# Expert weights in pieces of 16 KB to a partition, a ring of eight double places, and normalized rows stored permuted

## The chip, the cores and the metric

The kernel runs on one core of one Trainium2 chip. The metric is the device time of one execution in microseconds.

## The reference, cut to what matters

One transformer layer over 256 tokens of width 2048: three token mixers, a merge with `w_out` (2048 x 2048), a layer norm, a mixture of 16 experts of which each token takes two, and a second layer norm. The change concerns the experts and the first norm.

```python
x = layer_norm(ALPHA * x + mixed @ w_out, ln1_g, ln1_b)          # (256, 2048)
h = silu(einsum('td,edf->etf', x, w_gate)) * einsum('td,edf->etf', x, w_up)   # e = 16, f = 512
h = h * combine.T[:, :, None]                                    # two nonzero experts a token
x = layer_norm(ALPHA * x + einsum('etf,efd->td', h, w_down), ln2_g, ln2_b)
```

Each of `w_gate`, `w_up` (2048 x 512) and `w_down` (512 x 2048) is 4 MB an expert in fp32, so the experts are 192 MB in all (MB is 1,048,576 bytes here and below, where a weight is counted), and every byte is read once.

## The kernel before, in words

The engines run programs of their own and meet at semaphores. SP (`block.sync`) issues nearly all loads, in one fixed order on one queue, and waits before a load until its place is free; so whatever stands behind a waiting load waits too. PE (TensorE) multiplies, ACT (ScalarE) and DVE (VectorE) convert, normalize and add.

**The stages ahead of the experts.** Weights come as units of 1 MB (four rows of 512 columns to a partition, 2 KB each) into a ring `raw` of six slots. ACT rounds a unit to `whi` (line 1619), DVE takes the rest `wlo` (line 1866), PE multiplies three times (lines 1212 to 1214). `lo_done` counts converted units, `unit_used` multiplied ones. `whi` and `wlo` have two slots, so unit u is converted only when unit u - 2 has been multiplied. The 16 units of `w_out` are U1 to U1 + 15 (SP: lines 1093 to 1103, PE: lines 1568 to 1606, where n = u - U1). Between them SP puts in the first expert units, where a place is free by then (`first_units`, lines 406 to 418). DVE adds the residual into `xr` (line 978), storing each 512 columns permuted, so that a partition of a transposed tile holds rows p*4 + k; ACT then normalizes `xr` in place, in two activations (line 674). `gbT` holds the norm's gain and bias, transposed by PE at n = 4 (line 1595).

**The experts.** There are eight pairs of experts, in `step(m)` (line 537); six are written out, one is a loop that runs once with these inputs, and one is the last. An expert pair is 24 units of 1 MB (`expert_unit`, line 355): 16 of gate and up, four rows of 512 columns, which is 8 KB in one piece to a partition, and 8 of down, one row of 2048 columns, 8 KB too. In a pair PE gathers the tokens of both experts, 64 slots each (`gather`, line 510: q is a quarter of the 2048 columns), ACT copies them with gain and bias to `xg` (line 686), `gate_up(q)` (line 556) takes four units for a quarter q, gate and then up, ACT and DVE make `hh`, PE transposes it to `hT` (line 594), and the down product (line 646) takes two units for each quarter f of the 512 rows. `scatter` (lines 522, 523) adds the result of the pair before to the tokens. `m_used` counts used units; the order on PE is gather 0, 1, gate_up 0, gather 2, gate_up 1, gather 3, gate_up 2, 3, down.

**The places.** The first 20 units go to 20 places that come free in the `w_out` stage (`places`, line 231). After that, unit g waits until the unit that had its place before is used (lines 420 to 434). Three of the places (`once`: 14, 15, 16) are not used again, two more (`khT`, `qst`) join once `l1g` and `l1b` are consumed (`start_sum`, line 904), and the ring has 19 places. In the last pair the down units are quarters of columns, with pieces of 2 KB to a partition, and the last two come in halves of 1 KB pieces (`load_last`, line 401; used at line 617). SP's places in the order are lines 395 (a unit), 399 (half of a unit) and 404.

Of the kernel before, what the change touches and what calls it, by code (L numbers as in the profile page):

```python
# [20 lines left out]
P = 128  # L21
# [21 lines left out]
MRAW = 19  # L43
Z = 5
STEPS = 2 * GROUP
MU = 24
# [44 lines left out]
def build(nc, A, out):  # L91
# [14 lines left out]
    with ExitStack() as ctx:  # L106
# [116 lines left out]
        out_acc = at("out_acc", O2, [P, T, D])  # L223
# [10 lines left out]
        once = range(len(places), len(places) + 3)  # L234
        places += [O2, O2 + 8192, made["qbT"]]
        assert made["sig"] + 8192 <= made["cT"] + 2048
        places += [made[name] + (U1 + 15) % SPLIT * 8192 for name in ("whi", "wlo")]
        router_place = len(places)
        places.append(made["sig"])
        NP = len(places)  # L240
        places += [made["khT"], made["qst"]]
        mraw = [at(f"mraw{j}", o, [P, UNIT]) for j, o in enumerate(places)]
        second_round = [j for j in range(NP) if j not in once]
        GROWN = NP + len(second_round)
        ring = second_round[:4] + [NP, NP + 1] + second_round[4:]
        assert len(ring) == MRAW

        def place(g):
            if g < NP:
                return g  # L250
            return second_round[g - NP] if g < GROWN else ring[(g - GROWN) % MRAW]

        def user_before(g):
            return max((e for e in range(g) if place(e) == place(g)), default=None)

        LOOP0, LAST0 = (FIRST * MU - GROWN) % MRAW, (FIRST * MU + MU - GROWN) % MRAW
        L2R = MU - MRAW
        l2g, l2b, ysb = (at(n, places[ring[(LAST0 + L2R + j) % MRAW]], [P, D]) for j, n in enumerate(("l2g", "l2b", "ysb")))
# [28 lines left out]
        gb, gbT = at("gb", made["cT"], [2 * QUADS, 512]), carve(1, "gbT", [P, 2 * KT])  # L287
        wrg, wre = at("wrg", made["ddsa"], [P, KT, NG]), at("wre", made["dist"], [P, KT, NE])
# [9 lines left out]
        def sems(names):  # L298
# [33 lines left out]
        l1_in, l1_var, l1_std, l1_mul, z_ok, acc_ok, gb_in, gb_ps, gb_out = sems(  # L332
            "l1_in l1_var l1_std l1_mul z_ok acc_ok gb_in gb_ps gb_out")
# [21 lines left out]
        def expert_unit(r, pair, quarters=False):  # L355
# [7 lines left out]
            if quarters:  # L363
                c = (r - 4 * QUADS) // 2
                return A["expert_w_down"][0, bass.ds(e, 1), :, c * 512:(c + 1) * 512].rearrange("a (f p) n -> p (a f) n", p=P)
            kf = (r - 4 * QUADS) // 2
            return A["expert_w_down"][0, bass.ds(e, 1), kf * P:(kf + 1) * P, :].rearrange("a p d -> p a d")
# [4 lines left out]
        def loads_of(g):  # L372
            return 2 if NP <= g < NP + 4 else 1

        centre_order = (0, 5, 1, 2, 3, 6, 4, 7)

        def landed_value(r, m, turns):


            if m is not None:  # L380
                g = m * MU + r
                j = place(g)
                return j, mbase[j] + 16 * sum(loads_of(e) for e in range(g + 1) if place(e) == j)
            base = LOOP0 if turns[0] == "loop" else LAST0
            j = ring[(base + r) % MRAW]
            static = sum(loads_of(e) for e in range(FIRST * MU) if place(e) == j)
            turn = sum(1 for e in range(MU) if ring[(LOOP0 + e) % MRAW] == j)
            here = sum(1 for e in range(r + 1) if ring[(base + e) % MRAW] == j)
            return j, mbase[j] + 16 * (static + here) + turns[1] * (16 * turn)

        def load_unit(sp, r, pair, j, quarters=False):
            dst = mraw[j][:].unsqueeze(1)
            if quarters and r >= 4 * QUADS:
                dst = mraw[j][:].rearrange("p (f n) -> p f n", n=512)
            sp.dma_start(dst, expert_unit(r, pair, quarters)).then_inc(mlanded[j], 16)

        def load_half(sp, g, i):
            j, cols = place(g), slice(i * UNIT // 2, (i + 1) * UNIT // 2)
            sp.dma_start(mraw[j][:, cols].unsqueeze(1), expert_unit(g % MU, g // MU)[:, :, cols]).then_inc(mlanded[j], 16)

        def load_last(sp, r, i, signal):
            cols = slice(i * 256, (i + 1) * 256)
            dst = mraw[ring[(LAST0 + r) % MRAW]][:].rearrange("p (f n) -> p f n", n=512)
            sp.dma_start(dst[:, :, cols], expert_unit(r, PAIRS - 1, True)[:, :, cols]).then_inc(signal, 16)

        def first_units(sp, some):
            for r in some:
                if r < 4:
                    sp.wait_ge(unit_used, U1)
                elif r < 6:  # L410
                    sp.wait_ge(m_ps, 8)
                elif r < 6 + RAW:
                    sp.wait_ge(lo_done, U1 + 11 + r - 6)
                elif r == router_place:
# [1196 lines left out]
        def _(act):  # L1611
# [234 lines left out]
            for u in range(U1 + 2, U1 + 16):  # L1846
# [3 lines left out]
                if u == U1 + 2:  # L1850
                    merged(3)
# [295 lines left out]
```

## Time and profile before

| | us |
|---|---|
| median of 3 runs | 1325.91 |
| lowest, highest | 1325.45, 1325.94 |
| the profiled execution | 1324.61 |
| its span | 1322.9 |

PE is busy for 1308.2 us, which is 99% of the span, and its granted clock is full throughout. DVE is busy for 569.2 us and ACT for 476.6 us. The 40 slices of the page are 33 us each; the experts take the last 14. The DMA line is the busy share of the 16 DMA engines in tenths, the GB/s line what they moved. A span of the profiler and the device time of the same execution differ by 1.7 us here, which lies around the span.

### The profile page before, as it was taken

Reading aid. Unit: us, or ns where it says so; the run is one execution under the profiler, and the core shown is the slowest. Engines: PE = TensorE matmul, PEld = TensorE weight load, DVE = VectorE, ACT = ScalarE, POOL = GpSimd, SP = SyncE. Lnnn points to the kernel's source line nnn. Section 1 sums busy time; section 2 is a strip of 40 time slices with the busy share of each in tenths; the row PEclk is TensorE's granted clock in tenths of the full one; section 3 lists DMA queues with packets and bytes.
Section 4 is the critical chain, followed back from the end, with each engine's and each line's share of the span. In section 5 each row is a group of like instructions: output and inputs, shape, how many; then the busy total and the mean of one; then the engine's idle time right before and its main releaser. Section 6 shows DMA issues by size and latency. Waiting matters only on the chain.

```text
span 1322.9 us, 17951 instructions
## 1 busy us (share of the span) xinstructions
PE 1308.2 (99%) x7379; PEld 959.7 (73%) x7379; DVE 569.2 (43%) x741; ACT 476.6 (36%) x667; POOL 29.5 (2%) x55
## 2 busy tenths in 40 slices
PE   9999999999999999999999999999999999999998
PEld 9999989998888888888888888844453444544443
DVE  4367445356555644464455555525112121221206
ACT  4535343346556544454333433422121121211212
POOL 1000000400000000000100001000000000000000
PEclk9999999999999999999999999999999999999999
DMA  9965555544454445554556795699999999999996
GB/s 302 344 230 197 175 190 188 190 160 160 159 161 156 160 154 194 174 174 159 191 190 226 262 393 178 264 416 416 422 420 422 420 421 421 421 421 420 422 408 253
DMA packets 122100, 364.97 MB, mean 276 GB/s; under 512 B 11627, under 2 KB 19243, under 8 KB 98486
## 3 DMA queue, kind: packets, MB, share of 16 engines
q1 hardware_dynamic: 115430, 359.06, 73.1%
q10 hardware_dynamic: 6608, 5.02, 1.3%
q8 instruction: 47, 0.77, 0.2%
q14 instruction: 15, 0.12, 0.0%
HBM read 361.96 MB, written 2.10 MB: 275 GB/s over the span
## 4 chain that ended last, share of the span: by engine, by line
PE 93%; DMA 3%; DVE 2%; ACT 0%; issue 0%; SPq 0%; DVEq 0%; ACTq 0%
PE main L1212 19%; PE main L1214 19%; PE main L1213 19%; PE main L556 16%; PE att L646 7%; PE att L510 5%; DMA mraw<-in_expert_w_down_dram 3%; PE att L1453 1%; PE main L522 1%; PE main L523 1%; PE att L1436 1%; PE att L1472 1%; PE att L1468 1%; DVE wlo L1866 1%; PE att L1423 0%; PE att L617 0%
## 5 line engine op out<-in xcount | busy, mean ns | idle before, releaser
L1866 DVE TENSOR_TENSOR wlo<-raw,whi 128x2048 fp32r<-128x2048 f32 x135 | 310.3, 2299 | 360.3 <-ACT whi L1619 360.3
L1619 ACT ACTIVATE whi<-raw 128x2048 fp32r<-128x2048 f32 x135 | 258.1, 1912 | 420.4 <-PE main L1214 418.9
L556 PE MATMUL main<-mraw,xg 128*64 128x512 f32 x1024 | 225.4, 595 | 1.5 <-DMA mraw<-in_expert_w_up_dram 1.4
L1212 PE MATMUL main<-whi,xhi 128*128 128x512 f32 (+1 forms) x544 | 203.9, 375 | 0.0
L1214 PE MATMUL main<-whi,xlo 128*128 128x512 f32 (+1 forms) x544 | 201.7, 371 | 0.0
L1213 PE MATMUL main<-wlo,xhi 128*128 128x512 f32 (+1 forms) x544 | 201.6, 371 | 0.0
L556 PEld LDWEIGHTS main<-mraw,xg 128*64 128x64 f32 x1024 | 72.1, 137 | 137.4 <-issue 136.2
L1212 PE MATMUL main<-xhi,whi 128*128 128x256 f32 (+1 forms) x560 | 159.6, 285 | 1.1 <-DVE wlo L1997 1.0
L1213 PE MATMUL main<-xlo,whi 128*128 128x256 f32 (+1 forms) x560 | 158.4, 283 | 0.0
L1214 PE MATMUL main<-xhi,wlo 128*128 128x256 f32 (+1 forms) x560 | 158.4, 283 | 0.0
L1214 PEld LDWEIGHTS main<-whi,xlo 128*128 128x128 f32 x544 | 102.5, 188 | 17.7
L1213 PEld LDWEIGHTS main<-wlo,xhi 128*128 128x128 f32 x544 | 102.6, 189 | 17.2
L1212 PEld LDWEIGHTS main<-whi,xhi 128*128 128x128 f32 x544 | 102.6, 189 | 17.1
L1212 PEld LDWEIGHTS main<-xhi,whi 128*128 128x128 f32 (+1 forms) x560 | 106.9, 191 | 2.7 <-DVE xlo L1988 1.2
L1213 PEld LDWEIGHTS main<-xlo,whi 128*128 128x128 f32 (+1 forms) x560 | 106.9, 191 | 0.0
L1214 PEld LDWEIGHTS main<-xhi,wlo 128*128 128x128 f32 (+1 forms) x560 | 106.9, 191 | 0.0
L646 PE MATMUL att<-mraw,hT 128*64 128x512 f32 x448 | 98.1, 594 | 3.1 <-DMA mraw<-in_expert_w_down_dram 2.4
L686 ACT ACTIVATE xg<-att,gbT 128x128 f32<-128x128 f32 x128 | 47.3, 465 | 124.8 <-PE att L510 124.4
L646 PEld LDWEIGHTS att<-mraw,hT 128*64 128x64 f32 x448 | 31.6, 137 | 65.1 <-issue 60.9
L1212 PE MATMUL main<-whi,o 128*128 128x512 f32 x192 | 76.4, 398 | 0.0
L1214 PE MATMUL main<-whi,o 128*128 128x512 f32 x192 | 75.0, 391 | 0.0
L1213 PE MATMUL main<-wlo,o 128*128 128x512 f32 x192 | 74.8, 389 | 0.0
(336 smaller groups left out, 1300.8 us busy)
## 6 DMA issues: line engine op xcount, KB each, us to landing
raw<-in_w_in_dram SPq DMA_DIRECT2D x95, 1024.0 KB, 5.1
mraw<-in_expert_w_gate_dram SPq DMA_DIRECT2D x64, 1024.0 KB, 21.3
mraw<-in_expert_w_up_dram SPq DMA_DIRECT2D x64, 1024.0 KB, 22.4
mraw<-in_expert_w_down_dram SPq DMA_DIRECT2D x58, 1024.0 KB, 23.1
raw<-in_w_branch_dram SPq DMA_DIRECT2D x24, 1024.0 KB, 5.0
raw<-in_w_out_dram SPq DMA_DIRECT2D x16, 1024.0 KB, 7.9
mraw<-in_expert_w_down_dram SPq DMA_DIRECT2D x12, 512.0 KB, 9.3
xin<-in_x_dram SPq DMA_DIRECT2D x4, 512.0 KB, 8.2
```

What stands on the lines that cost most here:

```text
L510: ins = pe.matmul(att[:, q, k % 4 * P:(k % 4 + 1) * P], xr[:, t, k * P:(k + 1) * P], hot[:, t, :], start=(k % 4 == 0 and t == 0), stop=(t ...
L522: pe.matmul(o, rows, yhi[:, c % 2, :], start=True, stop=False)
L523: pe.matmul(o, rows, ylo[:, c % 2, :], start=False, stop=True).then_inc(sc_ps, 1)
L556: ins = pe.matmul(main[0][half, w, :], xg[:, k, half], src[:, kk * DE:(kk + 1) * DE], start=(k == 0), stop=(k == KT - 1))
L646: ins = pe.matmul(att[half, c, :], hT[:, f, half], src[:, c * 512:(c + 1) * 512], start=(f == 0), stop=(f == DE // P - 1))
L686: ins = act.activation(xg[:, k, :], att[:, q, k % 4 * P:(k % 4 + 1) * P], ACT.Identity, bias=gbT[:, KT + k:KT + k + 1], scale=gbT[:, k:k + 1])
L1212: pe.matmul(o, ah, bh, start=start, stop=False, skip_group_check=skip)
L1213: pe.matmul(o, ah, bl, start=False, stop=False, skip_group_check=skip)
L1214: return pe.matmul(o, al, bh, start=False, stop=stop, skip_group_check=skip)
L1436: ins = pe.transpose(att[:, seg, blk * P:(blk + 1) * P], sP[:, seg, blk * P:(blk + 1) * P], ident[:])
L1619: act.activation(whi[:, u % SPLIT, 0:n], raw[:, slot, 0:n], ACT.Copy).then_inc(hi_done, 1)
L1866: dve.tensor_tensor(wlo[:, u % SPLIT, 0:n], raw[:, slot, 0:n], whi[:, u % SPLIT, 0:n].bitcast(F32), ALU.subtract).then_inc(lo_done, 1)
```

## The change

An expert unit is now 2 MB: eight rows of 512 columns to a partition for gate and up, two rows of 2048 columns for down, in one piece of 16 KB. A pair has 12 units (`MU`), 8 of them gate and up (`GU`). The ring has eight double places; a double place is two of the old ones that lie side by side. `khT`, `qst`, the place at `sig` and the one at `qbT` are no longer in the ring. The first ten units fill the same 20 MB as before: five of them, and the first two of the ring's second turn, come in halves of 8 KB pieces (`load_half`), and unit 7 goes to where `xr` was, after the norm.

A unit of eight rows to a partition needs tokens in another order. ACT therefore normalizes `xr` into a new tensor `xn` (at the place of `mhi`), in eight activations of 512 columns that read with a stride; `out_acc` lies where `xr` was; and a second transposed gain and bias, `gbX`, is made: two small loads on SP ahead of U1 + 6, eight transposes on PE at n = 8, one copy on ACT. The small tensor `gbx` lies in place 5, so SP waits for the transposes before it loads unit 2. In a pair PE now uses all of gate before all of up within a half h: `gate_up(0)`, gather 2, gather 3, `gate_up(1)`. The down quarters of the last pair keep their shape.

```diff
-MRAW = 19
+RING = 8
-MU = 24
+MU = 12
+GU = 8
...
+        ring = [(0, 1), (2, 3), (4, 5), *((raw_at[n], raw_at[n + 1]) for n in range(0, RAW, 2)), *w_at]
+        first = [*ring[:7], (14, 15), ring[7], (16, 19)]
...
         def place(g):
-            if g < NP:
-                return g
-            return second_round[g - NP] if g < GROWN else ring[(g - GROWN) % MRAW]
+            return first[g] if g < NF else ring[(g - NF) % RING]
...
-            if r < 4 * QUADS:
-                q, name = r // 4, ("expert_w_gate", "expert_w_up")[r % 4 // 2]
-                rows = A[name][0, bass.ds(e, 1), q * 512:(q + 1) * 512, :]
+            if r < GU:
+                h, name = r // 4, ("expert_w_gate", "expert_w_up")[r % 4 // 2]
+                rows = A[name][0, bass.ds(e, 1), h * 1024:(h + 1) * 1024, :]
...
+            sp.wait_ge(z_ok, 2 * QUADS)
+            load_unit(sp, 7, 0, place(7))
+            sp.wait_ge(lt_out, 3)
+            for g in (NF, NF + 1):
+                load_half(sp, g, 0)
+            for g in (NF, NF + 1):
+                sp.wait_ge(m_used, user_before(g) + 1)
+                load_half(sp, g, 1)
+            for g in range(NF + 2, FIRST * MU):
+                sp.wait_ge(m_used, user_before(g) + 1)
                 load_unit(sp, g % MU, g // MU, place(g))
...
+                def gate_up(h):
+
                     for w in range(2):
+                        for kk in range(8):
+                            k = 8 * h + kk
+                            if kk % 4 == 0:
+                                if w == 0:
+                                    pe.wait_ge(xg_out, 1 + k // 4 + m * 4)
+                                for a in range(2):
+                                    arrived(4 * h + 2 * w + a, kk // 4)
...
-                                if kk == 3:
+                                if kk == 7:
                                     ins.then_inc(m_used, 1)
-                                elif kk == 1 and fixed == 0 and q == 0:
+                                elif kk == 3 and fixed == 0 and h == 0 and w == 0:
                                     ins.then_inc(lt_out, 1)
...
-                            if c == 3:
+                            if c == 3 and f % 2:
                                 ins.then_inc(m_used, 1)
...
-            for t in range(T):
-                act.activation(xr[:, t, :], xr[:, t, :], ACT.Identity, bias=nmr[:, t:t + 1],
-                               scale=rstd[:, t:t + 1]).then_inc(z_ok, 1)
+            for q in range(4):
+                half = slice(q // 2 * 1024, (q // 2 + 1) * 1024)
+                for t in range(T):
+                    src = xr[:, t, half].rearrange("p (c k m b) -> p b k c m", c=2, k=4, b=2)[:, q % 2]
+                    act.activation(xn[:, t, q * 512:(q + 1) * 512].rearrange("p (k c m) -> p k c m", k=4, c=2), src, ACT.Identity,
+                                   bias=nmr[:, t:t + 1], scale=rstd[:, t:t + 1]).then_inc(z_ok, 1)
...
+                    if u == U1 + 6:
+                        sp.wait_ge(m_ps, 8)
+                        for j, name in enumerate(("ln1_g", "ln1_b")):
+                            sp.dma_start(gbx[2 * j:2 * j + 2, :], A[name][0].rearrange("(h n) -> h n", h=2)).then_inc(gbx_in, 16)
                     if u in (U1 + 7, U1 + 9, U1 + 11):
-                        first_units(sp, range(u - U1 - 7, u - U1 - 5))
+                        g = (u - U1 - 7) // 2
+                        sp.wait_ge(unit_used, U1)
+                        if g == 2:
+                            sp.wait_ge(gb_ps, 2)
+                        load_unit(sp, g, 0, place(g))
...
+                    if n == 8:
+                        pe.wait_ge(gbx_in, 32)
+                        pe.wait_ge(gb_out, 1)
+                        for k in range(8):
+                            ins = pe.transpose(att[:, 2, 128 + k * 4:128 + (k + 1) * 4],
+                                               gbx[:].rearrange("r (m k) -> r k m", k=8)[:, k, :], ident[0:4, 0:4])
+                        ins.then_inc(gb_ps, 1)
```

Two places of the order show what moves. The first is SP's queue in the `w_out` stage, ahead of and behind the load of the unit at U1 + 11; `mraw` and `mtwo` are the old and the double places, `raw` the ring of the `w_out` units. Before:

```order
L395 DMA mraw_136<-in_expert_w_up_dram 128x2048 [waits unit_used]
L395 DMA mraw_137<-in_expert_w_up_dram 128x2048 [waits unit_used]
L1048 DMA raw<-in_w_out_dram 128x4x512 [waits lo_done] x2
L395 DMA mraw_138<-in_expert_w_gate_dram 128x2048 [waits m_ps]
L395 DMA mraw_139<-in_expert_w_gate_dram 128x2048 [waits m_ps]
L1048 DMA raw<-in_w_out_dram 128x4x512 [waits lo_done] x5
```

After the change:

```order
L1132 DMA gbx<-in_ln_g_dram 2x1024 [waits m_ps]
L1132 DMA gbx<-in_ln_b_dram 2x1024
L1077 DMA raw<-in_w_out_dram 128x4x512 [waits lo_done]
L402 DMA mtwo_143<-in_expert_w_gate_dram 128x4096 [waits unit_used]
L1077 DMA raw<-in_w_out_dram 128x4x512 [waits lo_done] x2
L402 DMA mtwo_144<-in_expert_w_gate_dram 128x4096 [waits unit_used]
L1077 DMA raw<-in_w_out_dram 128x4x512 [waits lo_done] x2
L402 DMA mtwo_145<-in_expert_w_up_dram 128x4096 [waits gb_ps,unit_used]
L1077 DMA raw<-in_w_out_dram 128x4x512 [waits lo_done] x5
```

The five last `w_out` loads now stand behind a load that waits for `gb_ps`, which PE raises to 2 behind its eight new transposes at n = 8; before, the load ahead of them waited for `m_ps` alone.

The second place is SP's queue at the start of the experts, from the first load that waits for a multiply of the experts. Before:

```order
L399 DMA mraw_134<-in_expert_w_down_dram 128x1024 [waits lt_out]
L399 DMA mraw_135<-in_expert_w_down_dram 128x1024 [waits lt_out]
L399 DMA mraw_134<-in_expert_w_down_dram 128x1024 [waits m_used]
L399 DMA mraw_135<-in_expert_w_down_dram 128x1024 [waits m_used]
L399 DMA mraw_136<-in_expert_w_down_dram 128x1024 [waits lt_out]
L399 DMA mraw_137<-in_expert_w_down_dram 128x1024 [waits lt_out]
L399 DMA mraw_136<-in_expert_w_down_dram 128x1024 [waits m_used]
L399 DMA mraw_137<-in_expert_w_down_dram 128x1024 [waits m_used]
L395 DMA mraw_138<-in_expert_w_gate_dram 128x2048 [waits m_used]
L395 DMA mraw_139<-in_expert_w_gate_dram 128x2048 [waits m_used]
```

After the change:

```order
L402 DMA mtwo_150<-in_expert_w_up_dram 128x4096 [waits z_ok]
L406 DMA mtwo_143<-in_expert_w_down_dram 128x2048 [waits lt_out]
L406 DMA mtwo_144<-in_expert_w_down_dram 128x2048
L406 DMA mtwo_143<-in_expert_w_down_dram 128x2048 [waits m_used]
L406 DMA mtwo_144<-in_expert_w_down_dram 128x2048 [waits m_used]
L402 DMA mtwo_145<-in_expert_w_gate_dram 128x4096 [waits m_used]
L402 DMA mtwo_146<-in_expert_w_gate_dram 128x4096 [waits m_used]
```

The waits are of the same kind, but each now stands for twice the bytes, and `m_used` is raised half as often.

## Rows read from the trace of the kernel before

**Rows 1.** The page: GB/s in 40 slices; DMA issues, KB each, median us to landing.

```profile
GB/s 302 344 230 197 175 190 188 190 160 160 159 161 156 160 154 194 174 174 159 191 190 226 262 393 178 264 416 416 422 420 422 420 421 421 421 421 420 422 408 253
...
mraw<-in_expert_w_gate_dram SPq DMA_DIRECT2D x64, 1024.0 KB, 21.3
...
raw<-in_w_branch_dram SPq DMA_DIRECT2D x24, 1024.0 KB, 5.0
```

**Rows 2.** Windows: PE, PEld, DVE, ACT, POOL busy (instructions), PEclk, DMA share, GB/s.

```profile
868.00:1280.00 412.00, 407.66 (x2102) 183.08 (x2098) 84.92 (x169) 73.63 (x193) 0.00 (x0) 1.00 1.01 420
1060.00:1160.00 100.00, 99.83 (x522) 45.99 (x520) 21.10 (x46) 20.12 (x52) 0.00 (x0) 1.00 1.01 421
1286.00:1292.00 6.00, 4.97 (x23) 1.84 (x21) 2.02 (x4) 1.46 (x5) 0.00 (x0) 1.00 1.05 387
```

**Rows 3.** Waits of PE from 820 us on: engine, line, releaser, us, times, longest.

```profile
PE att L646 <- DMA mraw<-in_expert_w_down_dram: 2.4, 2, 1.4
PE att L617 <- DMA mraw<-in_expert_w_down_dram: 1.4, 2, 0.9
PE main L556 <- DMA mraw<-in_expert_w_up_dram: 1.4, 1, 1.4
```

**Rows 4.** Chain of waits, first two pairs: start, us, engine, tile, line, count.

```profile
863.63 7.02 PE main L556 x32
870.65 1.98 PE att L510 x16
872.63 7.02 PE main L556 x32
...
882.19 13.93 PE main L556 x64
...
898.08 13.95 PE att L646 x64
...
918.57 7.02 PE main L556 x32
```

**Rows 5.** Timeline of SP's DMA issues around the last `w_out` units: start, span, count.

```profile
784.99 23.81 SPq L1048 DMA_DIRECT2D raw<-in_w_out_dram  x5
813.95 6.51 SPq L395 DMA_DIRECT2D mraw<-in_expert_w_up_dram  x2
...
852.09 0.81 SPq L395 DMA_DIRECT2D mraw<-in_expert_w_up_dram  x2
852.94 3.07 SPq L395 DMA_DIRECT2D mraw<-in_expert_w_down_dram  x4
```

**Rows 6.** Chain of waits in the `w_out` stage: start, us, engine, tile, line, count.

```profile
786.07 0.57 PE att L1595 x4
...
809.51 0.57 PE att L1561 x8
...
821.20 0.87 PE att L1552 x8
```

**Rows 7.** Timeline of ACT and of DVE: conversion of unit U1 + 10.

```profile
809.61 1.92 ACT L1619 ACTIVATE whi<-raw 128x2048 fp32r<-128x2048 f32 x1 [3.52 <-PE main L1214]
...
811.64 2.27 DVE L1866 TENSOR_TENSOR wlo<-raw,whi 128x2048 fp32r<-128x2048 f32 x1
```

**Rows 8.** Timeline of ACT ahead of the first pair: normalization, tables, first `xg`.

```profile
855.20 4.08 ACT L674 ACTIVATE xr<-xr,nmr,rstd 128x2048 f32<-128x2048 f32 x2 [0.43 <-DVE nmr L1017]
...
861.88 1.50 ACT L686 ACTIVATE xg<-att,gbT 128x128 f32<-128x128 f32 x4 [0.82 <-PE att L510]
```

**Rows 9.** Timeline of PE in the last pair, from its last gate/up units on.

```profile
1281.83 3.65 PE L556 MATMUL main<-mraw,xg 128*64 128x512 f32 x16 [1.36 <-DMA mraw<-in_expert_w_up_dram]
...
1288.12 3.65 PE L617 MATMUL att<-mraw,hT 128*64 128x512 f32 x16 [0.80 <-ACT hT L702]
1292.68 3.65 PE L617 MATMUL att<-mraw,hT 128*64 128x512 f32 x16 [0.91 <-DMA mraw<-in_expert_w_down_dram]
...
1297.98 3.65 PE L617 MATMUL att<-mraw,hT 128*64 128x512 f32 x16 [0.51 <-DMA mraw<-in_expert_w_down_dram]
```

More of the change, by code:

```diff
@@ L242, in build @@
[L242 to L246, printed above, removed]
+        raw_at = {(places[j] - made["raw"]) // 8192: j for j in range(6, 6 + RAW)}
+        w_at = [(12, 17), (13, 18)] if places[12] < places[17] else [(17, 12), (18, 13)]
+        ring = [(0, 1), (2, 3), (4, 5), *((raw_at[n], raw_at[n + 1]) for n in range(0, RAW, 2)), *w_at]
@@ new lines, in build, with half_of @@
+        first = [*ring[:7], (14, 15), ring[7], (16, 19)]
+        assert len(ring) == RING and all(places[a] + 8192 == places[b] for a, b in ring + first[:9])
+        NF = len(first)
+        IN_HALVES = (5, 6, 8, 9, NF, NF + 1)
+        doubles = {a: at(f"mtwo{a}", places[a], [P, 2 * UNIT]) for a, _ in ring + first[:9]}
+        singles = [at(f"mraw{j}", places[j], [P, UNIT]) for j in first[9]]
+        def half_of(where, i):
+            return singles[i][:] if where == first[9] else doubles[where[0]][:, i * UNIT:(i + 1) * UNIT]
@@ L248, in place @@
         def place(g):
-            if g < NP:
-                return g
-            return second_round[g - NP] if g < GROWN else ring[(g - GROWN) % MRAW]
+            return first[g] if g < NF else ring[(g - NF) % RING]
         def user_before(g):
[L254 to L258, printed above, removed]
+            return max(e for e in range(g) if place(e) == place(g))
@@ L259, in build @@
+        LOOP0, LAST0 = (FIRST * MU - NF) % RING, (FIRST * MU + MU - NF) % RING
+        L2R = GU // 2
+        l2g, l2b, ysb = (at(n, places[j], [P, D]) for n, j in zip(
+            ("l2g", "l2b", "ysb"), (*ring[(LAST0 + L2R) % RING], ring[(LAST0 + L2R + 1) % RING][0])))
         small = [made["ksT"], made["pT"]]
@@ L380, in landed_value @@
+        def landed_value(r, m, turns, half):
             if m is not None:
                 g = m * MU + r
[L382 to L387, printed above, removed]
@@ L401, in load_last @@
[L401 to L414, printed above, removed]
-                    sp.wait_ge(r_ps, T)
-                else:
-                    sp.wait_ge(unit_used, U1 + 4 * QUADS - (1 if r < 8 + RAW else 0))
-                load_unit(sp, r, 0, r)
@@ new lines, in landed_value @@
+                return j, mbase[j] + 16 * sum(signals(e, j) for e in range(g + 1))
+            last = turns[0] == "last"
+            base = LAST0 if last else LOOP0
+            j = ring[(base + r) % RING][half if last and r >= GU else 0]
+            static = sum(signals(e, j) for e in range(FIRST * MU))
+            turn = sum(1 for e in range(MU) if ring[(LOOP0 + e) % RING][0] == j)
+            here = sum(1 for e in range(r + 1) if ring[(base + e) % RING][half if last and e >= GU else 0] == j)
@@ new lines, in tile, with arrived @@
+                def tile(r, half):
+                    if fixed is not None:
+                        return half_of(place(fixed * MU + r), half)
+                    return half_of(ring[((LAST0 if turns[0] == "last" else LOOP0) + r) % RING], half)
+                def arrived(r, half):
+                    if half == 0 or (fixed is not None and fixed * MU + r in IN_HALVES):
+                        landed_, value = unit(r, half)
+                        pe.wait_ge(landed_, value)
+                def gate_up(h):
+                    for w in range(2):
+                        for kk in range(8):
[3 more added lines that the diff above has]
+                                    pe.wait_ge(xg_out, 1 + k // 4 + m * 4)
+                                for a in range(2):
+                                    arrived(4 * h + 2 * w + a, kk // 4)
```

169 lines of the change are left out of this document (87 added, 82 removed).

## The prediction

> **What bounds the kernel now.** I read the DMA line of the page first. Its last 14 slices are the experts, and from the 27th on it stands at 416 to 422 GB/s, where the stages before move 154 to 393 [rows 1]. The windows say the same in one number: from 868 to 1280 us the DMA engines are at a share of 1.01 and move 420 GB/s, 421 in the middle [rows 2]. But PE is busy for 407.7 of the same 412 us. The waits of PE decide between the two: from 820 us on PE waits for weights five times, 5.2 us in all, all of it late (up units, down units, last quarters) [rows 3]. The chain of waits gives the pace of PE: a pair begins `gate_up(0)` at 863.63, the next at 918.57, so a pair needs 54.9 us of PE [rows 4]. A pair is 24 MB; at 421 GB/s that is 24 x 2.491 = 59.8 us of DMA. **So the stage is bound by DMA, and PE lives for five pairs on the 20 MB loaded ahead of it.** The DMA queue never ran dry: a unit lands 21.3 us after its issue, against the 2.5 us that it takes [rows 1]. The last gate/up unit lands at 1281.83, and behind it the quarters come so closely that PE waits before the second and the third [rows 9]. What happens to DMA between about 868 and 1282 is therefore what the change is worth, plus what it puts on PE ahead of that.
>
> A difference below 0.2% (2.65 us) can't be told from no change here.
>
> **Term 1, the piece of 16 KB.** Pieces of 8 KB run at 421 GB/s and those of 2 KB in the last pair at 387 [rows 2]. By engine that is 16 x 8192 / 421 = 311.3 ns and 16 x 2048 / 387 = 84.7 ns a piece: 36.9 ns for each 1000 bytes and 9.2 ns fixed. A piece of 16 KB should take 613.4 ns, against 622.6 for two, which is 427 GB/s and 0.037 us less a MB. Bounds: nothing (a long piece is cut in two, or costs in proportion), and the rate with no fixed cost at all, 434 GB/s (0.075 us a MB). I take the fit, since it goes through the nearest rows. Of the 164 MB that come after the first 20 and up to the last gate/up unit, 160 have 16 KB pieces: 160 x 0.037 = **-5.9 us** (0 to -12).
>
> The Trainium skill (DMA: Bandwidth & Descriptors, Why small descriptors are slow) gives the fixed cost as about 3 cycles a packet, and elsewhere on the page a fabric clock of 850 MHz, which makes an estimate of 3.5 ns; the rows above show 9.2. By the page's figure this term would be -2.3 us and the sum 3.6 us higher; the measured one decides.
>
> **Term 2, the queue runs dry.** A load waits until its place is used. Before, places of 1 MB come free two at a time each 3.5 us, of 19. Now they come free 4 MB at a time each 7 us, of 16, and unit 7, the one at `sig` and the one at `qbT` are out of the ring. I walk through the first two pairs in the time of before. PE's marks are from the chain [rows 4]: `gate_up(0)` from 863.63 for 14.04 (both old parts), `gate_up(1)` from 882.19 for 13.93, down from 898.08 for 13.95, next pair from 918.57. A place is known free 0.13 us after the multiply (865.38 by the chain, 865.52 on SP). A load on an empty queue starts 1.0 us later: a 1 MB unit lands 5.0 us after its issue [rows 1] and takes 2.7 at 2 KB pieces, so 2.3 us lie at its two ends, of which I give the start a bit less than half (0 to 2.3). It shifts every restart alike and changes the sum of the gaps little. A MB takes 2.52 us over the whole stretch (164 MB from 868.2 to 1281.83; the code loads and restarts are in it), so with the new pieces 2.483, and a double unit 4.97.
>
> The first 20 MB end at 868.2, as before: three units from 852.09 on, a fourth with `r_ps`, and unit 7 behind the norm (about 860) still find the queue busy until then [rows 5, 8]. Then, with the release and the start of each:
> - units 10, 11, first halves: released at 867.14, start 868.3, gap 0.2; with the second halves (870.65) they end at 878.4.
> - 12, 13: released at 877.67 (up used), start 878.8, gap 0.4, end 888.7.
> - 14, 15: 889.16, start 890.3, gap 1.6, end 900.2. Unit 16 (896.12): no gap, end 905.2.
> - 17: waits for down, 905.05, gap 1.0, end 911.2.
> - 18, 19: 912.03, gap 2.0, end 923.1.
> - 20, 21: 925.59, gap 3.6, end 936.6. From 22 on (932.6) the releases lead, since PE is the faster.
>
> Sum: **+8.8 us** of lost DMA time, which a stage bound by DMA never gets back. PE doesn't feel it there: units 12, 13 are needed at 918.57. Bounds: 0, if the places come as early as before; 12, if each of the six restarts costs 0.5 us more.
>
> **Term 3, the w_out stage.** PE has eight more transposes at n = 8. Four cost 0.57 us [rows 6], so +1.1. And SP now waits for them before unit 2 and the five last `w_out` loads. Before, these five were issued from 784.99 on, though the first of them (U1 + 11) is needed late [rows 5]. Now: n = 8 ends at 809.51 [rows 6], the transposes at 810.65, unit 2 starts at 811.8 and takes 4.9, the unit U1 + 11 takes 2.7 at 387 GB/s and lands at 819.4; ACT needs 1.92, DVE 2.27 [rows 7], so PE can start n = 11 at 823.8. It would be there at 822.07 (821.20 + 0.87) + 1.1 = 823.2 [rows 6]. That is +0.6, **together +1.8** with 0.1 for two more semaphores. Both shift the later marks of PE, the releases and the DMA alike. Bounds: +1.1 and, if the load is 3 us later than I reckon, +4.7. The wait for `m_ps` ahead of U1 + 6 holds loads that have 20 us to spare.
>
> **Term 4, the end.** PE takes 7.0 us for up of both experts after the last 4 MB have landed, not 3.65 for the last 2 MB [rows 9]: +3.35. In exchange the waits before the second and third quarter, 0.9 and 0.5, vanish, for the quarters land 5.4 us apart: **+1.9**. Bounds: 0 and 3.4.
>
> **Edits at nothing.** The norm in eight pieces: 4.08 us as two [rows 8], perhaps 4.7 as eight, until 859.9; the first gather waits for the token table and starts at 859.86 in any case, and ACT has 0.8 us free before its first `xg` [rows 8]. If the stride cost double, PE would be late by about 3 us once. The other order of gather 3, the strided transposes of `hh`, `gbX`, the sum in four pieces on DVE: beside a busy PE, or four small weight loads a pair. Half as many issues on SP: it waits anyway.
>
> **Sum:** -5.9 + 8.8 + 1.8 + 1.9 = +6.6 us. The profiled execution (1324.61, span 1322.9) would go to 1331.2, span 1329.5; the median shown is 1.3 us above it, so 1325.91 + 6.6 = 1332.5.
>
> **Rivals.**
> - *The piece of 16 KB brings nothing.* Term 1 is 0, the gaps shrink by 0.6: 1337.8. For: no load of before has such a piece. Against: the fixed cost shows from 2 to 8 KB. 17%.
> - *The queue doesn't run dry.* If releases or starts come sooner, so that the gaps stay near zero, as before, term 1 wins: 1332.5 - 8.8 = 1323.7, the border of faster. It decides from a gap sum below about 0.3 us. Against: the rows of the chain leave no room for six such gaps to close. 12%.
> - *A transfer of double size runs much faster,* and DMA is no longer the bound. Then PE waits for nothing: -6.2 (the 5.2 of rows 3 and what follows from them in the last two pairs) + 1.8 = -4.4, 1321.5. This needs over 439 GB/s from a fit that ends at 434, or both this and smaller gaps. 6%.
> - *The late `w_out` load costs more* (upper bound of term 3): 1335.4. 8%.
> - *Terms cancel:* gaps half as long, rest as reckoned: about 1328. 7%.
>
> The third is what a rule of the Trainium skill would give (the same page, Bandwidth: batch to at least 1 MB, 78% of the peak there and 97% at 16 MB); the 21.3 us in the queue against 2.5 us of moving show that the fixed cost of a load is hidden already.
>
> **Numbers.** The forecast has 50%, its own range is 1329 to 1336. The range of 8 in 10 takes in the first rival, and the second in part: 1325 to 1339. Faster by over 0.2% (below 1323.3): the third rival and half of the second, 12%. Within 0.2%: the rest of the second, the last one, 15%. Slower: 73%.
>
> **What would show it.** DMA share below 1 in windows between 878 and 927, later at 1.01 with about 427 GB/s; a wait of PE before n = 11; waits for weights already in the sixth pair; seven us of up after the last wait for gate/up. Wrong if the GB/s line holds 420 or more from the start of the experts on, or if the rate of the middle is 421 or less.

## The result, and the profile after

| us | before | after |
|---|---|---|
| median | 1325.80 (4 runs) | 1336.32 (4 runs) |
| lowest, highest | 1325.45, 1325.94 | 1336.04, 1336.93 |
| the profiled execution | 1324.61 | 1336.19 |
| its span | 1322.9 | 1334.5 |

The changed kernel is slower by 10.5 us: the ratio is 1.008, with a 95% interval from 1.0063 to 1.0098. The forecast was 1332.5 with a range of 1325 to 1339. The sign and this range hold; the narrower one, 1329 to 1336, is missed by 0.3, and the sum of +6.6 is 3.9 us short. I look for those 3.9 us first, and then ask whether the terms that fit the total also fit their places.

**The rate.** Two lines of the page after (GB/s in 40 slices of 33.4 us; a gate load with KB and us to landing), to be held against [rows 1]:

```profile
GB/s 305 345 219 205 177 192 188 170 170 165 164 163 145 169 157 158 183 194 156 190 189 258 193 280 258 311 380 351 423 428 427 427 427 429 426 427 428 426 410 225
...
mtwo<-in_expert_w_gate_dram SPq DMA_DIRECT2D x31, 2048.0 KB, 22.1
```

The middle of the experts runs at 426 to 429 GB/s where it ran at 420 to 422, and ahead of it stand a 380, a 351 and a 423 where before had 416, 416 and 422. Windows put the same in stretches of equal length. The window of before over its first 70 us of the experts (us; PE, PEld, DVE, ACT, POOL busy; PEclk; DMA share; GB/s):

```profile
863.00:933.00 70.00, 68.82 (x358) 30.40 (x358) 23.88 (x43) 14.92 (x39) 0.00 (x0) 1.00 1.01 417
```

and those of the changed kernel: the same stretch of its experts, the middle, and some short ones to which I come below.

```profile
870.00:940.00 70.00, 68.38 (x351) 29.72 (x352) 23.62 (x39) 13.31 (x35) 0.00 (x0) 1.00 0.93 365
1060.00:1160.00 100.00, 97.96 (x495) 43.83 (x492) 19.05 (x37) 17.04 (x43) 0.00 (x0) 1.00 1.01 428
...
810.88:812.88 2.00, 2.00 (x15) 1.32 (x8) 2.00 (x3) 0.95 (x1) 0.00 (x0) 1.00 0.68 123
812.88:814.88 2.00, 2.00 (x11) 1.65 (x10) 1.37 (x1) 0.00 (x0) 0.00 (x0) 1.00 0.85 344
810.88:822.15 11.27, 11.27 (x56) 9.00 (x49) 3.37 (x3) 0.95 (x1) 0.00 (x0) 1.00 0.91 339
...
826.00:830.00 4.00, 3.55 (x10) 2.86 (x11) 3.59 (x4) 1.68 (x2) 0.00 (x0) 0.59 1.05 388
...
1252.00:1254.00 2.00, 2.00 (x9) 0.78 (x7) 0.00 (x0) 0.00 (x0) 0.00 (x0) 0.64 1.04 442
1254.00:1256.00 2.00, 2.00 (x6) 0.61 (x4) 0.00 (x0) 0.00 (x0) 0.00 (x0) 0.51 0.96 410
```

The DMA share falls to 0.93 in the first 70 us. At 417 GB/s instead of 365, 3.64 million bytes more would have gone through, which is 8.7 us of DMA; term 2, the dry queue, had 8.8. And 428 against 421 is term 1: 0.04 us a MB.

**The w_out stage.** The waits of PE from 700 us on (engine, line, releaser: us, times, longest):

```profile
PE att L672 <- DMA mtwo<-in_expert_w_down_dram: 8.9, 5, 2.8
PE main L1249 <- DVE wlo L1915: 3.1, 1, 3.1
PE main L581 <- DMA mtwo<-in_expert_w_up_dram: 1.7, 1, 1.7
...
PE main L581 <- ACT xg L715: 0.9, 1, 0.9
```

The second row is new: PE stands still for 3.1 us before n = 11, in a stage that had no such wait in [rows 3]. The chain of waits tells how it came about (start, us, engine, tile, line, count):

```profile
809.82 0.98 PE att L1639 x8
810.88 0.34 SPq L402
811.26 10.87 DMA raw<-in_w_out_dram
822.15 1.93 ACT whi L1663
824.10 2.30 DVE wlo L1915
826.45 0.80 PE main L1249
827.24 0.43 PE main L1250
827.67 0.43 PE main L1251
...
870.44 13.96 PE main L581 x64
```

It reads from the top: the eight new transposes (0.98), SP's issue of unit 2, then the load of the `w_out` unit U1 + 11, which lands 10.87 us after 811.26; ACT and DVE convert it in 4.3 us; PE goes on at 826.45. And the matmuls behind it stand 0.43 us apart, where the same three lines stand 0.23 apart before the wait: the window from 826 to 830 has a granted clock of 0.59, after PE had been idle for 3.1 us. That is the lower level of 1.2 GHz for most of the stretch, where before had the full clock throughout. The Trainium skill (TensorE: Matmul & The Clock Gate, Wait — 56ns, not 53.3ns?) gives 426.7 ns from matmul to matmul at 512 columns and 1.2 GHz; the 0.43 agrees.

On SP the wait that causes it has a row of its own (queue, line, releaser: us, times, longest):

```profile
SPq L1137 <- PE att L1639: 30.6, 1, 30.6
```

SP has nothing to do for 30.6 us but wait for the transposes. Of the five loads behind it, four have time; U1 + 11 has not. The activations of the norm in the same kernel (timeline of ACT):

```profile
861.20 6.09 ACT L703 ACTIVATE xn<-xr,nmr,rstd 128x512 f32<-128x512 f32 x8 [0.43 <-DVE nmr L1046]
```

take 6.09 us as eight, where two took 4.08 [rows 8], and PE waits 0.9 for the first `xg`.

**The end.** The timeline of PE in the changed kernel, seventh and last pair:

```profile
1251.38 8.78 PE L672 MATMUL att<-mtwo,hT 128*64 128x512 f32 x32 [2.70 <-DMA mtwo<-in_expert_w_down_dram]
...
1284.84 13.95 PE L581 MATMUL main<-mtwo,xg 128*64 128x512 f32 x64
```

Thirty-two matmuls take 8.78 us instead of the 7.09 that this group takes elsewhere. The windows from 1252 to 1256 say why: granted clock 0.64 and 0.51, after an idle time of 2.70. In the last pair PE then finds the 64 gate/up matmuls of its second half all supplied.

### The profile page after: what moved, and what is told of

It reads as the page before. It is cut to its first block, busy times and chain, and to the rows that moved or that the text cites. A ratio compares the mean times of both kernels' runs of the same rounds, so it can differ in the third digit from the quotient of the medians.

```text
span 1334.5 us, 17804 instructions
## 1 busy us (share of the span) xinstructions
PE 1310.8 (98%) x7387; PEld 967.7 (73%) x7387; DVE 569.1 (43%) x737; ACT 478.4 (36%) x674; POOL 29.5 (2%) x55
## 4 chain that ended last, share of the span: by engine, by line
PE 88%; DMA 8%; DVE 2%; ACT 1%; issue 0%; SPq 0%; DVEq 0%; ACTq 0%
PE main L1249 19%; PE main L1251 18%; PE main L1250 18%; PE main L581 14%; DMA mtwo<-in_expert_w_down_dram 7%; PE att L672 6%; PE att L524 3%; PE att L1490 1%; PE main L536 1%; PE att L644 1%; PE main L537 1%; DMA raw<-in_w_out_dram 1%; DVE wlo L1915 1%; PE att L1473 1%; PE att L1509 1%; PE att L1505 1%
## 5 line engine op out<-in xcount | busy, mean ns | idle before, releaser
L581 PE MATMUL main<-mtwo,xg 128*64 128x512 f32 x1024 | 223.8, 594 | 2.9 <-DMA mtwo<-in_expert_w_up_dram 1.7
L581 PEld LDWEIGHTS main<-mtwo,xg 128*64 128x64 f32 x1024 | 74.1, 137 | 141.3 <-issue 140.1
L672 PE MATMUL att<-mtwo,hT 128*64 128x512 f32 x432 | 100.0, 603 | 9.3 <-DMA mtwo<-in_expert_w_down_dram 8.9
L715 ACT ACTIVATE xg<-att,gbX 128x128 f32<-128x128 f32 x128 | 47.2, 464 | 121.3 <-PE att L524 120.9
L672 PEld LDWEIGHTS att<-mtwo,hT 128*64 128x64 f32 x432 | 33.9, 139 | 70.5 <-issue 67.3
```

The source lines that it names most:

```text
L581: ins = pe.matmul(main[0][half, w, :], xg[:, k, half], src[:, kk % 4 * DE:(kk % 4 + 1) * DE], start=(k == 0), stop=(k == KT - 1))
L672: ins = pe.matmul(att[half, c, :], hT[:, f, half], src[:, c * 512:(c + 1) * 512], start=(f == 0), stop=(f == DE // P - 1))
L715: ins = act.activation(xg[:, k, :], att[:, q, k % 4 * P:(k % 4 + 1) * P], ACT.Identity, bias=gbX[:, KT + k:KT + k + 1], scale=gbX[:, k:k + 1])
```

## The experiments

Nine kernels were run, one of them twice, each beside the kernel before on the same chip, whose medians were 1325.65, 1325.51 and 1325.57 in the three groups of runs. My theory was that the total is made of the four terms, with term 3 larger than I had put it and the clock as its hidden part; the rivals were a slower norm, a useless piece size, and a queue that fell dry for another reason than places and releases.

**1. Unit 2 later: the wait off the path.** SP loads unit 2, and waits for the transposes, only behind the last `w_out` load.

```diff
         def moe_loads(sp):
+            sp.wait_ge(gb_ps, 2)
+            load_unit(sp, 2, 0, place(2))
             sp.wait_ge(lo_done, U1 + 11)
...
-                    if u in (U1 + 7, U1 + 9, U1 + 11):
+                    if u in (U1 + 7, U1 + 9):
...
-                        if g == 2:
-                            sp.wait_ge(gb_ps, 2)
```

> The changed kernel, with the load of expert unit 2 and its wait for the new transposes put behind the last w_out load instead of ahead of five of them. Theory (SP's wait holds the w_out weights; what PE loses there is lost to the end, since the release of places and the norm shift with it): the wait of PE of 3.1 us before n = 11 goes, and so do the slow matmuls behind it (about 1.4 us); the first gate product starts near 866 instead of 870.4; time 1336.3 - 4.5 = 1331.8. Rival (the experts are bound by DMA, so a late start of PE costs nothing while DMA is fed): 1336. Second rival (loading unit 2 later only moves the loss): above 1335, with a late unit 2 or a longer dry queue.

Measured: 1330.93 (1329.96 to 1331.38), ratio 1.0042 (1.0028 to 1.0056); run once more in a later group it gave 1330.09 (1329.82 to 1330.67), ratio 1.0036 (1.0022 to 1.0050).

> The kernel of e1_unit2_late once more, on the same chip as e5_late_flat, to compare the two directly. 1330.9 as before, by every theory; a difference of more than 1 us would say how far runs on another chip carry.

The wait for `wlo` is gone, the first gate product starts at 865.63 instead of 870.44, and the first 70 us still run at 366 GB/s:

```profile
865.00:935.00 70.00, 68.20 (x349) 29.59 (x350) 23.79 (x40) 13.49 (x35) 0.00 (x0) 1.00 0.93 366
```

So the order of SP's loads in the `w_out` stage costs about half of what the change costs, and the dry queue has nothing to do with it. The timeline of PE shows the end of this kernel too:

```profile
1187.51 8.78 PE L674 MATMUL att<-mtwo,hT 128*64 128x512 f32 x32 [2.92 <-DMA mtwo<-in_expert_w_down_dram]
...
1246.24 7.09 PE L674 MATMUL att<-mtwo,hT 128*64 128x512 f32 x32 [2.04 <-DMA mtwo<-in_expert_w_down_dram]
...
1285.46 7.09 PE L583 MATMUL main<-mtwo,xg 128*64 128x512 f32 x32 [0.33 <-DMA mtwo<-in_expert_w_up_dram]
```

The first row is the low clock again, behind a wait of 2.92 us; it cost nothing there, since PE had to wait for the next down units all the same (2.04). Here PE does wait in the last pair's up, and has 7.09 us of it after the last 4 MB have landed. From that mark to the end of the span (1328.2) there are 42.7 us; before, from 1281.83 [rows 9] to 1322.9, there were 41.1. That is term 4, +1.7 for a forecast of +1.9, where it was said to be.

**2. The same wait in the kernel before.** Only this is added to before:

```diff
                             sp.dma_start(x_of(j), A["x"][0, :, j * 512:(j + 1) * 512].rearrange("(t p) d -> p t d", p=P)).then_inc(xr_in, 16)
+                    if u == U1 + 11:
+                        sp.wait_ge(unit_used, U1 + 9)
```

> The kernel before with one wait added: SP waits until PE has done n = 8 before it loads units 4, 5 and the w_out unit U1 + 11. Theory (the wait alone makes PE wait about 3 us before n = 11 and then run about 1.4 us at the lower clock, and this is lost to the end): 1325.8 + 4.4 = 1330.2. Rival (DMA bound, a late PE costs nothing): 1325.8. Rival (the later loads of units 4 and 5 also hold the next loads): above 1332.

Measured: 1330.75 (1329.38 to 1331.41), ratio 1.0038 (1.0025 to 1.0052). The windows, then the chain of waits of this kernel:

```profile
809.63:811.63 2.00, 2.00 (x15) 1.32 (x16) 1.97 (x3) 1.92 (x1) 0.00 (x0) 1.00 0.43 78
811.63:813.63 2.00, 2.00 (x10) 1.66 (x9) 2.00 (x2) 0.00 (x0) 0.00 (x0) 1.00 1.00 414
...
826.00:830.00 4.00, 4.00 (x11) 3.17 (x10) 3.29 (x3) 0.53 (x1) 0.00 (x0) 0.50 1.08 399
870.00:940.00 70.00, 68.82 (x356) 30.08 (x354) 23.14 (x39) 14.41 (x37) 0.00 (x0) 1.00 1.01 415
```

```profile
825.28 0.80 PE main L1214
826.07 0.43 PE main L1215
...
831.16 0.23 PE main L1215
...
869.81 7.02 PE main L556 x32
```

One wait on SP, with no other part of the change, moves the first gate product by 6.2 us (863.63 in [rows 4]) and the time by 5.1. The profiled execution is one of the longer ones: its span is 6.6 us over that of before. By the timeline, from the first matmul of n = 11 to the fifteenth pass 6.0 us here (825.28 to 831.23) and 3.3 in before (821.83 to 825.10). So the clock adds 2.7 us to an idle time of the same 3.1 us as in the changed kernel, where it added 1.4 (3.3 us from the first to the ninth, 1.9 in before). The DMA share is 1.01 in the first 70 us: no dry queue with 19 fine places.

**3. Pieces of 8 KB in the changed kernel.** Each 2 MB unit is loaded by two DMAs of 8 KB pieces to the same place; the counts of landed loads follow.

```diff
...
-            sp.dma_start(doubles[where[0]][:].unsqueeze(1), expert_unit(r, pair)).then_inc(mlanded[where[0]], 16)
+            for i in range(2):
+                cols = slice(i * UNIT, (i + 1) * UNIT)
+                sp.dma_start(half_of(where, i).unsqueeze(1), expert_unit(r, pair)[:, :, cols]).then_inc(mlanded[where[0]], 16)
```

> The changed kernel with each 2 MB unit loaded by two DMAs with pieces of 8 KB; places, waits and order unchanged. Theory (a piece has a fixed cost of about 9 ns, worth 0.037 us a MB): rate in the middle 421 GB/s instead of 428, the units of the last pairs land 5 to 6 us later, time 1341.5. Rival (the size of the piece has no part in it): 1336.3. Rival the other way (smaller loads fill the queue better at the start and win back some of the gaps): 1334 to 1336.

Measured: 1340.58 (1340.01 to 1341.06), ratio 1.0113 (1.0097 to 1.0128); that is 0.0033 above the changed kernel's ratio, 4.4 us.

```profile
870.00:940.00 70.00, 68.19 (x349) 29.56 (x350) 23.79 (x40) 13.49 (x35) 0.00 (x0) 1.00 0.93 366
1060.00:1160.00 100.00, 94.80 (x479) 43.24 (x477) 19.07 (x37) 17.05 (x43) 0.00 (x0) 1.00 1.01 422
```

The rate of the middle goes back to 422, while the first 70 us move 366 GB/s as with long pieces: where the queue waits for places, the long piece gains nothing. And PE's waits for down and up grow from 8.9 and 1.7 to 11.5 and 3.5. The long piece is worth what the two rates say: 160 MB x 0.035 us is 5.6, of which 4.4 to 4.8 (spans 1339.3 against 1334.5) arrive. The first rival is out.

**4. Sixteen places, release by fours, and both, in the kernel before.** First `MRAW = 16`, with the ring's list cut accordingly (`ring = second_round`); then 19 places, but a load waits until the group of four units is used:

```diff
-                    sp.wait_ge(m_used, user_before(g) + 1)
+                    sp.wait_ge(m_used, user_before(g) // 4 * 4 + 4)
```

and then both.

> The kernel before with a ring of 16 places of 1 MB instead of 19 (the place at sig is used once, khT and qst never). Theory (capacity alone makes the DMA queue run dry in the first two pairs): gaps of 4.6 us in sum, the largest near 920 us, none after 930; time 1325.7 + 4.4 = 1330.1. Rival (the gaps of the change come from places being given back 4 MB at a time alone): no gap, 1325.7.

> The kernel before with its 19 places, but from the fifth unit behind the first 20 on SP waits until all four units of a quarter (or of two down rows) are used, so places come free 4 MB at a time. Theory (coarse release alone costs gaps too, but less than half): gaps of 2.7 us near 880 and 906 us, time 1325.7 + 2.5 = 1328.2. Rival (release alone is the cause): 1334. Rival (19 places hide it): 1325.7.

> The kernel before with both: 16 places and release by fours; pieces stay at 8 KB and the w_out stage is untouched. Theory (capacity and release together are the changed kernel's dry queue): gaps of 8.1 us, time 1325.7 + 7.9 = 1333.6, more than either alone. Rival (the two overlap, the larger one decides): 1330.

Measured: 1328.73 (1328.25 to 1329.29), ratio 1.0025 (1.0015 to 1.0035); 1328.31 (1327.74 to 1329.60), ratio 1.0021 (1.0012 to 1.0031); both together 1333.62 (1331.93 to 1334.57), ratio 1.0057 (1.0044 to 1.0071). The windows over the first 70 us of sixteen places:

```profile
864.00:934.00 70.00, 68.82 (x356) 30.09 (x356) 23.24 (x40) 14.48 (x37) 0.00 (x0) 1.00 0.97 390
```

of release by fours:

```profile
864.00:934.00 70.00, 68.82 (x356) 30.13 (x356) 23.47 (x41) 14.53 (x37) 0.00 (x0) 1.00 0.99 395
```

and of both:

```profile
863.00:933.00 70.00, 68.82 (x359) 30.52 (x359) 23.94 (x43) 15.04 (x39) 0.00 (x0) 1.00 0.93 369
```

Against 417 these are 4.5, 3.7 and 8.1 us of DMA, where I expected gaps of 4.6, 2.7 and 8.1; the time of sixteen places, expected at 1330.1, came out 1.4 us lower. In the timeline the last down product of the seventh pair starts at 1241.13 in before, at 1245.73, 1245.39 and 1250.91 here: +4.6, +4.3 and +9.8, so what the queue loses stands whole at that mark. In the windows the two losses add (4.5 + 3.7 against 8.1); at the mark and in the time both together cost more than the sum of the single ones (9.8 against 8.9, and 8.1 against 6.0). About half of the latter has a reason. Of a loss about 1 us is not seen in the time (+3.2 and +2.8 for the single ones), because before itself loses about 1 us between that mark and the last up units: 40.7 us pass between the two there (1241.13 to 1281.83), 39.75 with sixteen places (to 1285.48). That 1 us is hidden twice in the sum of the single ones and once in both together; the rest of the difference stays open. The dry queue is thus half capacity, half granularity, and with both it is nearly as large as in the changed kernel (8.1 against 8.7).

**5. Release by halves in the changed kernel.** Experiment 1, and the first 16 units of the ring's turns come in halves of 8 KB pieces, each loaded when its half of the place is used (a new semaphore `half_used` at the fourth of eight steps).

```diff
-        IN_HALVES = (5, 6, 8, 9, NF, NF + 1)
+        IN_HALVES = (5, 6, 8, 9, *range(NF, NF + 16))
...
+            for g0 in range(NF, NF + 16, 2):
+                for i, used in enumerate((half_used, m_used)):
+                    for g in (g0, g0 + 1):
+                        sp.wait_ge(used, user_before(g) + 1)
+                        load_half(sp, g, i)
```

> The changed kernel with unit 2 loaded late (as e1_unit2_late), and in the first two pairs of the ring (units 10 to 25) loads of 1 MB that start as soon as half a unit is used; from unit 26 on double units as in the change. Theory (finer release fills about half of the gaps, for 32 MB at the 8 KB rate): gaps 4.7 instead of about 8.8 us, time 1330.9 - 3.1 = 1327.8. Rival (capacity alone counts): 1331. Rival (twice the waits and issues on SP eat it): above 1331.

Measured: 1327.79 (1326.76 to 1329.45), ratio 1.0017 (1.0008 to 1.0026).

```profile
865.00:935.00 70.00, 68.39 (x351) 29.72 (x352) 23.61 (x39) 13.34 (x35) 0.00 (x0) 1.00 0.96 385
1060.00:1160.00 100.00, 99.83 (x522) 46.65 (x520) 21.11 (x46) 20.16 (x52) 0.00 (x0) 1.00 1.01 428
```

385 instead of 366 GB/s is 3.2 us of DMA, and 3.1 are gone from the time (2.3 by the second run of experiment 1). The middle keeps its 428, since long pieces matter only where the queue is full. What is left of the gaps is 5.4 us by the window; sixteen places alone cost 4.5 in experiment 4, and the rest I did not take apart. This is the fastest version of the changed kernel that I ran, and before is still faster by 2.3 us.

**6. The norm without the permutation.** Eight activations of 512 columns, read and written in order, once in the changed kernel and once on top of experiment 1. The result is then not the layer's, since the columns of the tokens meet the wrong weight rows; the loads and multiplies stay the same.

```diff
-                half = slice(q // 2 * 1024, (q // 2 + 1) * 1024)
+                cols = slice(q * 512, (q + 1) * 512)
...
-                    act.activation(xn[:, t, q * 512:(q + 1) * 512].rearrange("p (k c m) -> p k c m", k=4, c=2), src, ACT.Identity,
+                    act.activation(xn[:, t, cols], xr[:, t, cols], ACT.Identity,
```

> The changed kernel, with the eight activations of the norm reading and writing 512 columns in a row, without the permutation (so the columns of the tokens meet the wrong weight rows; all else as before). Theory (the strided read costs ACT 160 ns an activation, and PE 0.9 us at the first gate product): each activation 0.6 us instead of 0.76, the eight 4.8 instead of 6.1, no wait of PE for xg, time 1335.4. Rival (hidden, since DMA bounds): 1336.3. Other rival (the norm's end also holds unit 7, so more): 1334.5.

> e1_unit2_late and e2_flat_norm together: unit 2 loaded behind the last w_out load, and the norm without the permutation (the columns of the tokens meet the wrong weight rows). It asks again what the strided norm costs, without the wait of PE in the w_out stage, which alone varied by 1.1 us between the profiles. Theory (the stride costs PE 0.9 us at the first gate product and nothing later): 1330.9 - 0.9 = 1330.0, no wait for xg. Rival (hidden, since DMA bounds): 1330.9. Rival (the norm's end also delays unit 7 and with it the queue): 1329.

Measured: 1335.48 (1332.81 to 1336.65), ratio 1.0071 (1.0057 to 1.0085), and 1329.65 (1329.41 to 1331.19), ratio 1.0035 (1.0023 to 1.0048), beside 1330.09 for experiment 1 on the same chip. The timeline of ACT in the second of them:

```profile
856.38 5.75 ACT L704 ACTIVATE xn<-xr,nmr,rstd 128x512 f32<-128x512 f32 x8 [0.43 <-DVE nmr L1047]
```

The stride costs 0.34 us in all, the cutting into eight 1.67 (5.75 against 4.08). I had expected 160 ns an activation for the stride; it is 43 ns. PE still waits 0.53 us for `xg`, 0.3 less than with the stride, and the 0.4 us between the medians can't be told from the spread of the runs. The first of the two is inconclusive as a time, and that it met the expected 1335.4 is luck: its wait before n = 11 was 4.2 us in the profiled execution, and its runs spread over 3.8 us. But its timeline of PE has two rows that matter for the clock and the end:

```profile
1252.80 7.09 PE L672 MATMUL att<-mtwo,hT 128*64 128x512 f32 x32 [2.70 <-DMA mtwo<-in_expert_w_down_dram]
...
1292.03 7.09 PE L581 MATMUL main<-mtwo,xg 128*64 128x512 f32 x32 [0.36 <-DMA mtwo<-in_expert_w_up_dram]
```

The same wait as in the changed kernel at the same place, 2.70 us, and the clock stayed full; 39.2 us later the last up units have landed, as in experiment 1 (1246.24 to 1285.46), and PE has waited for them.

## Why the prediction was right or wrong

**What bounds the kernel: right.** Every DMA loss that I made stood whole at the end of the seventh pair (experiment 4), and of the 5.6 us of rate taken away in experiment 3, 4.4 to 4.8 came out in the time. The signs named came too: the DMA share fell, PE waited before n = 11, and it waited for weights even a pair earlier than said, in the fifth (at 1132.34).

**Term 1, the piece of 16 KB, -5.9: right.** 428 GB/s against a forecast of 427, or 612.5 ns a piece against 613.4; taken away, it costs 4.4 to 4.8 us. The fixed cost that I fitted from pieces of 2 and 8 KB, 9.2 ns, holds at 16. The 3 cycles of the Trainium skill (DMA: Bandwidth & Descriptors, Why small descriptors are slow), 3.5 ns in my estimate, would have made the term -2.3; experiment 3 decides for the fit.

**Term 2, the dry queue, +8.8: right,** 8.7 by the windows. The cause was also the one of the walk, too few places and too coarse releases, each of which gives about half alone. The places of the gaps fit as well: the widest one of the walk, from 923.1 to 926.7, moved by the 6.8 us that PE is later, is 929.9 to 933.5, and the windows of the changed kernel there are

```profile
928.44:930.44 2.00, 2.00 (x12) 0.69 (x10) 0.00 (x0) 0.00 (x0) 0.00 (x0) 1.00 0.83 352
930.44:932.44 2.00, 2.00 (x12) 0.60 (x10) 0.00 (x0) 0.00 (x0) 0.00 (x0) 1.00 0.08 33
932.44:934.44 2.00, 2.00 (x12) 0.72 (x10) 0.00 (x0) 0.00 (x0) 0.00 (x0) 1.00 0.80 156
```

The second rival (no gaps) is out.

**Term 3, the w_out stage, is the step that failed: "+0.6, together +1.8" is 6.8.** The first gate product starts at 870.44 and not 863.63. By the chain: 0.3 was there already ahead of the stage (786.38 for the transposes at n = 4, against 786.07); the eight transposes are 1.0, as forecast (1.1); the wait for `wlo` puts n = 11 another 3.3 us later, where I had 0.6; the low clock behind it adds 1.4, where I had nothing; the norm and the wait for `xg` add 0.8, which I had under "edits at nothing" as 0.6 us of ACT that would hide.

Two sizes are wrong. First, the landing of U1 + 11: I had unit 2 and the next load run at full rate from the first microsecond (819.4). It landed at 822.15. The idle queue started slowly: 123 and 344 GB/s in the first four microseconds, against some 420 that is 1.8 us of DMA, of which I had 0.9. And by 822.15 DMA had moved 3.6 MB (339 GB/s for 11.27 us), though unit 2 and U1 + 11 are 3: the loads issued behind U1 + 11 took their share of the engines before it was complete. Second, I priced a wait of PE by its length alone. A full-clock kernel has no row that shows what PE does after an idle time of 3 us, and I didn't ask what it would cost if the clock fell. The range did hold "the load 3 us later", +4.7, as the fourth rival; with the clock and the norm behind it, it is 6.8. Experiment 2 shows the wait and the clock of this term without the transposes and the norm, at +5.1 in time; experiment 1 takes these two away, 4.8 us at the first gate product (870.44 to 865.63), and gives back 5.4 and 6.2.

**Term 4, the end, +1.9: right, but the end has a part more.** Experiment 1 and the flat norm show it where it was said to be, +1.7. In the changed kernel's profiled execution there is no wait in the last pair, because PE came late itself: the clock fell once more behind the 2.70 us at 1251.38, and cost 1.7 us (8.78 for 7.09). Only a part of that took the place of waiting. With 39.2 us from this mark to the landing of the last up units, as in experiment 1 and the flat norm, they landed at about 1290.6 here, while PE starts its second half of up at about 1291.8 (1284.84 and half of 13.95). So 1.2 us of the second fall are in the time of this execution, and the prediction has no term for them. After 1291.8 it is 42.7 us to the end of the span, as in experiment 1. "Seven us of up after the last wait for gate/up" was therefore not to be seen.

**The sum.** Against the marks, the last up of the last pair is +10.0 (1291.8 against 1281.83). It is made of 6.8 for term 3, 8.7 for term 2, 1.2 for the second fall of the clock and, as what is left, -6.7. Of that the rate gives 5.6: the 8.7 is counted at the old rate, and long pieces gain nothing in the first 70 us, so some 140 of the 164 MB are left at 0.04 us. The other 1 us is about what before loses ahead of its last up units (40.7 against 39.75 in experiment 4), which fits but was not tested. After the mark it is +1.6, together the 11.6 by which the spans differ, where I had +6.6. Against the forecast, term 3 is 5.0 too small and the second fall 1.2, which I had put at nothing; terms 1 and 2 together are +2.0 for +2.9, and term 4 is 0.3 less. The medians show 3.9 of the missing 5.0, since the before of the profiled execution was 1.2 us under its median and the after only 0.1. The mechanism holds but for the clock, and that the total lies in the wide range owes something to its width: term 3 alone lies 2.1 us above its own bound.

**What stays open.** The eight transposes on PE (1.0) and the wait for `xg` (0.9) were never taken away together with the gaps. A ninth double place, from `khT` and `qst`, was not tried; neither was a kernel that keeps 19 fine places for the first two pairs and takes 16 KB pieces from the third on, which by my estimate from these terms would lose only term 4, the transposes and the norm's part. Why the clock fell behind some waits of 2.7 us and not behind others is open too.

## What to carry to other kernels

A larger transfer pays only while its queue is full; price it together with the places and the moments at which they come free, since a ring of eight places of 2 MB instead of nineteen of 1 MB ran dry for 8.7 us here against 5.6 gained; fewer bytes and coarser release had about half each. When a new wait goes into a queue in fixed order, look at the most urgent load behind it, and give a load on an idle queue its slow start. And price a new stall on TensorE with what the granted clock does after it: 3.1 us idle cost 4.5 and 5.8 us in two kernels.

## What the runs showed of the hardware that was not expected

- After 3.1 us without work the granted clock fell to its lower level, for 1.4 us of lost time in one kernel and 2.7 in another. Behind somewhat shorter waits it fell in half of the cases. The profiled executions of the changed kernel and its variants have twelve waits of 2.7 to 2.9 us ahead of a down product; behind six of them the 32 matmuls took 8.78 us, behind the other six 7.09. In the changed kernel it fell behind 2.70 us at 1251.38 and not behind 2.76 at 1192.64, in experiment 1 behind 2.92 at 1187.51, in the flat norm behind neither of its two waits of 2.70. After three waits of 2.0 us it did not fall. A wait of this length is thus a risk with a spread. Of the five runs of experiment 2 the fastest, 1329.38, has a mean granted clock of 1.000 and the others 0.997 to 0.999. It is not the only source of spread: the five runs with 16 places and release by fours all have 1.000 and differ by 2.6 us.
- An idle DMA queue starts slowly, with pieces of either size: from the first issue on 123, then 344 GB/s in two stretches of 2 us with pieces of 16 KB, 78 and 414 with pieces of 8 KB in experiment 2. That is 1.8 and 1.7 us lost against 420. And a load is not complete when its bytes' turn is over: the load of U1 + 11 landed after 3.6 MB had moved for the 3 issued up to it.
- PE's weight loads from the permuted `hh`, read with a stride, have a median of 196 ns against 140 (32 of them, 4 a pair, so 0.2 us a pair); I saw no mark moved by it.
